# Seven half-size products in place of eight for three weight groups of a hybrid layer, with the sums done by VectorE

## What is computed

```python
h = rmsnorm(x, norm_w)
proj = jnp.matmul(h, w_in).astype(jnp.float32)     # 256x1024 times 1024x4360
...
(aq, ak, av, ag, bq, bk, bv, bg, cq, ck, cv, co, cg, ci, cf) = jnp.split(proj, cuts, axis=-1)
...
qk = jax.nn.silu(causal_dwconv(jnp.concatenate([cq, ck], axis=-1), conv_w, conv_b))
...
yc = mlstm(split_heads(cq_c, C_HEADS), split_heads(ck_c, C_HEADS), split_heads(cv, C_HEADS),
           i_pre, f_pre)
yc = yc * split_heads(jax.nn.sigmoid(co), C_HEADS)
```

## Time and profile before

| | |
|---|---|
| median of 3 runs | 1400.82 us (1400.11 to 1401.28) |
| profiled execution | 1402.55 us, span 1400.4 us |
| TensorE busy | 1197.1 us, 85% |
| VectorE busy | 604.2 us, 43% |
| ScalarE busy | 209.9 us, 15% |

### The profile page before, as it was taken

The page is one execution under the profiler, slowest core; times in us unless marked ns, Lnnn a source line. Parts: engine busy times, 40 slices in busy tenths (PEclk is TensorE's granted clock), DMA queues, the critical chain, the costliest instruction groups (busy, mean ns, idle before and its releaser), DMA issues.

```text
span 1400.4 us, 27434 instructions
## 1 busy us (share of the span) xinstructions
PE 1197.1 (85%) x10062; PEld 607.4 (43%) x10063; DVE 604.2 (43%) x1355; ACT 209.9 (15%) x474; POOL 49.4 (4%) x84
## 2 busy tenths in 40 slices
PE   7999999999999989976877779887799987878665
PEld 6757577665674433422333323333234432323222
DVE  1436333454587535433443334444354543334323
ACT  1214021130262201101110111101110110101001
POOL 0000000001011000000000000000000000000000
PEclk9999999999999999988999989999999998999888
DMA  9942177221833999999999999999979999999996
GB/s 351 282 138 91 61 280 138 78 92 59 299 145 125 380 410 418 426 429 429 427 427 430 428 428 428 426 429 428 428 306 429 429 429 428 427 430 428 429 428 288
DMA packets 63075, 467.79 MB, mean 334 GB/s; under 512 B 6848, under 2 KB 11708, under 8 KB 38460
## 3 DMA queue, kind: packets, MB, share of 16 engines
q1 hardware_dynamic: 58556, 462.49, 80.1%
q10 hardware_dynamic: 3856, 2.65, 2.3%
q0 software_dynamic: 624, 2.10, 0.4%
HBM read 465.12 MB, written 1.05 MB: 333 GB/s over the span
## 4 chain that ended last, share of the span: by engine, by line
PE 55%; DMA 34%; DVE 4%; issue 3%; SPq 2%; ACT 1%; ACTq 1%; POOLq 0%; POOL 0%; DVEq 0%
DMA ring<-in_w_up_dram 29%; PE bank L1406 18%; PE bank L978 9%; PE bank L985 7%; PE bank L1437 6%; PE bank L1154 3%; DMA ring<-in_w_down_dram 2%; PE bank L1454 2%; PE bank L1387 2%; DMA x_mem<-x_mem 1%; SPq L503 1%; PE bank L1350 1%; PE bank L1418 1%; PE bank L1211 1%; ACTq L920 1%
## 5 line engine op out<-in xcount | busy, mean ns | idle before, releaser
L1406 PE MATMUL bank<-ring,mem 128*32 128x512 f32 x2688 | 378.3, 657 | 123.0 <-DMA ring<-in_w_up_dram 100.4
L1406 PEld LDWEIGHTS bank<-ring,mem 128*32 128x32 f32 x2688 | 103.0, 119 | 306.5 <-issue 246.6
L978 PE MATMUL bank<-ring 128*128 128x256 f32 x768 | 168.7, 380 | 0.0
L1437 PE MATMUL bank<-ring,mem 128*32 128x256 f32 x2560 | 155.1, 382 | 8.4 <-DMA ring<-in_w_down_dram 7.9
L978 PEld LDWEIGHTS bank<-ring 128*128 128x128 f32 x768 | 145.1, 190 | 21.1 <-issue 1.7
L935 ACT ACTIVATE const<-bank 64x512 f32<-64x512 f32 x46 | 27.3, 594 | 795.2 <-PE bank L1406 795.2
L2440 DVE TENSOR_TENSOR mem<-bank,const 64x512 f32<-64x512 f32 x45 | 30.7, 683 | 228.5 <-PE bank L1406 228.5
L985 PE MATMUL bank<-ring 128*128 128x512 f32 (+2 forms) x320 | 123.6, 542 | 1.5 <-DVE ring L1745 1.3
L1437 PEld LDWEIGHTS bank<-ring,mem 128*32 128x32 f32 x2560 | 75.3, 109 | 77.1 <-issue 26.8
L1406 PE MATMUL bank<-x_mem,mem 128*32 128x512 f32 x256 | 69.3, 689 | 29.8 <-DMA ring<-in_w_up_dram 29.8
L985 PEld LDWEIGHTS bank<-ring 128*128 128x128 f32 x320 | 61.0, 195 | 55.8 <-issue 49.6
(11 more groups left out here) (421 smaller groups left out, 1160.5 us busy)
## 6 DMA issues: line engine op xcount, KB each, us to landing
ring<-in_w_up_dram SPq DMA_DIRECT2D x64, 2048.0 KB, 28.7
ring<-in_w_gate_dram SPq DMA_DIRECT2D x54, 2048.0 KB, 32.1
ring<-in_w_down_dram SPq DMA_DIRECT2D x53, 2048.0 KB, 26.7
ring<-in_w_in_dram SPq DMA_DIRECT2D x19, 2048.0 KB, 13.1
x_mem<-in_w_gate_dram SPq DMA_DIRECT2D x10, 2048.0 KB, 31.6
x_mem<-in_w_down_dram SPq DMA_DIRECT2D x10, 2048.0 KB, 28.3
ring<-in_w_out_dram SPq DMA_DIRECT2D x6, 2048.0 KB, 14.3
ring<-in_w_in_dram SPq DMA_DIRECT2D x2, 1056.0 KB, 6.4
```

Of the source, the lines that this page charges most:

```text
L978: i = mm(b[:, S * j:S * j + S], w[:, k, P * (c + j):P * (c + j + 1)], hT[:, k, :], start=(k == 0), stop=(k == KC - 1))
L1406: i = mm(gate_up_bank(q), xT[:, at:at + T], w[q // 2][:, c, 512 * (q % 2):512 * (q % 2 + 1)], start=(h == 0 and c == 0 and not begun), sto ...
L1437: i = mm(YB[quarter[q], 0:QD], hT_sb[:, at:at + T], w[:, c, cols_of[q]], start=(h == 0 and c == 0), stop=(h == 1 and c == 3), skip_group_c ...
```

## The change

Groups 1, 2 and 4 are each cut in halves along the tokens, the contraction and the columns of weights. The product of two such 2x2 block matrices is made with seven half-size products instead of eight (Winograd's form of Strassen's scheme). Each half-size product is 128 tokens by 512 of the contraction by 256 columns. For groups 1 and 2 it is eight matmuls that stream 128 tokens; for group 4 it is four matmuls that stream 256 columns.

VectorE makes, once a layer, four sums of halves of `hT` (`s1` to `s4`); for each group four sums of weight blocks in the ring itself (`mix`, T3, T2, T1, T4, each 128x1024 numbers) and five sums of products on their way out of PSUM (`fold`, 128x256 numbers each). ScalarE keeps three products a group (`keep`). For group 2 these operations stand inside of the gate chain. For group 4 they stand between the gate chain and the wait for the spread rows. On TensorE the first two state scores and two more pieces of group 5 change places with each other.

```diff
+SEVEN = {g: n for n, g in enumerate((1, 2, 4))}
+PRODUCTS = {name: n + 1 for n, name in enumerate(("M1", "M3", "M7", "M6", "M5", "M2"))}
+KEPT = {name: n + 1 for n, name in enumerate(("M1", "M3", "C11"))}
+FOLDED = {name: n + 1 for n, name in enumerate(("U2", "U4", "C22", "C12", "C21"))}
+MIXED = {name: n + 1 for n, name in enumerate(("T3", "T2", "T1", "T4"))}
...
+        s1, s2 = four(flat2(agT))[:, :, 0:P], four(flat2(agT))[:, :, P:S]
+        s3, s4 = four(flat2(vgB))[:, :, 0:P], four(flat2(vgB))[:, :, P:S]
+        u4 = mem3[:, 0:S]
+        products_of = {1: rawC[:, :, 3:3 + S], 2: qkA[:, 0:4, :]}
+        scale_of = {1: 1.0, 2: SCALE, 4: 1.0}
+        def corner(g, i, j):
+            if g == 4:
+                return eC[:, i, 0:S].rearrange("p (h d) -> p h d", d=HD) if j else vC[:, i, :, 0:HD]
+            return products_of[g][:, 2 * j:2 * j + 2, P * i:P * (i + 1)]
+        def chunks_of(b, g=1):
+            return b[:, 0:S].rearrange("p (c s) -> p c s", c=4 if g == 4 else 2)
+        def weights_of(g, k, n):
+            w = ring[:, g % SLOTS, :].rearrange("p (k n) -> p k n", n=512)
+            return w[:, 4 * k:4 * k + 4, S * n:S * (n + 1)]
...
+                def keep(g, product, dst, b):
+                    act.wait_ge(product_ready, seven(PRODUCTS, l, g, product))
+                    A(dst, chunks_of(b, g), ACT.Copy, scale=scale_of[g]).then_inc(kept, 1)
+                def keep_first(g):
+                    keep(g, "M1", corner(g, 1, 0), PJ[2 * g % 4])
+                    keep(g, "M3", corner(g, 0, 1), PJ[(2 * g + 1) % 4])
+                def keep_corner(g):
+                    keep(g, "M2", corner(g, 0, 0), PJ[2 * g % 4])
+                    act.sem_inc(pj_used, 2)
+                keep_first(1)
+                keep_corner(1)
+                keep_first(2)
                 arg(1)
                 result(A(rw[:, 3, :], rw[:, 2, :], ACT.Exp))
                 arg(2)
                 result(A(rw[:, 5, :], rw[:, 4, :], ACT.Ln))
-                for c in range(2):
-                    b = unit(4 + c)
-                    used(A(qkA[:, 2 * c:2 * c + 2, :], b[:, :].rearrange("p (c s) -> p c s", c=2), ACT.Copy, scale=SCALE))
-                    if c == 0:
-                        arg(3)
-                        result(A(eg[:, :, :], qkC[:, :, :], ACT.Tanh, scale=0.5))
+                keep_corner(2)
...
+                keep_first(4)
+                keep(4, "M2", corner(4, 0, 0), PJ[0])
+                for c, name in enumerate(("C12", "C22")):
+                    act.wait_ge(folded, seven(FOLDED, l, 4, name))
+                    used(A(eC[:, c, 0:S], eC[:, c, 0:S], ACT.Tanh, scale=0.5))
...
-                group(1, "T")
+                def seven_products(g):
+                    a, m, f, e = PJ[2 * g % 4], PJ[(2 * g + 1) % 4], SC[1], SC[0]
+                    hT0, hT1 = hT[:, :, 0:P], hT[:, :, P:S]
+                    def product(name, b, w, moving, first=True):
+                        for k in range(4) if g == 4 else ():
+                            i = mm(b[:, 0:S], moving[:, k, :], w[:, k, :], start=(first and k == 0), stop=(k == 3),
+                                   skip_group_check=True)
+                        for j in range(2) if g < 4 else ():
+                            for k in range(4):
+                                i = mm(b[:, P * j:P * (j + 1)], w[:, k, P * j:P * (j + 1)], moving[:, k, :],
+                                       start=(first and (j, k) == (0, 0)), stop=(k == 3), skip_group_check=True)
+                        return i.then_inc(product_ready, 1) if name in PRODUCTS else i.then_inc(pj_ready, 2)
+                    arrived(g, l * in_loads[g] + 1)
+                    if g == 1:
+                        pe.wait_ge(sc_used, l * SC_L)
+                    elif g == 2:
+                        pe.wait_ge(pj_used, l * PJ_L + 2)
+                        pe.wait_ge(folded, seven(FOLDED, l, 1, "C21"))
+                    else:
+                        pe.wait_ge(kept, seven(KEPT, l, 2, "C11"))
+                        pe.wait_ge(folded, seven(FOLDED, l, 2, "C21"))
+                    product("M1", a, weights_of(g, 0, 0), hT0[:, 0:4, :])
+                    pe.wait_ge(sums_ready, 4 * l + 3)
+                    product("M3", m, weights_of(g, 1, 1), s4)
+                    pe.wait_ge(sums_ready, 4 * l + 4)
+                    pe.wait_ge(mixed, seven(MIXED, l, g, "T3"))
+                    product("M7", f, weights_of(g, 0, 1), s3)
+                    pe.wait_ge(kept, seven(KEPT, l, g, "M3"))
+                    pe.wait_ge(mixed, seven(MIXED, l, g, "T2"))
+                    product("M6", m, weights_of(g, 0, 0), s2)
+                    pe.wait_ge(mixed, seven(MIXED, l, g, "T1"))
+                    product("M5", e, weights_of(g, 1, 1), s1)
+                    product("M2", a, weights_of(g, 1, 0), hT0[:, 4:8, :], first=False)
+                    pe.wait_ge(folded, seven(FOLDED, l, g, "C22"))
+                    pe.wait_ge(mixed, seven(MIXED, l, g, "T4"))
+                    product("M4", f, weights_of(g, 0, 1), hT1[:, 4:8, :], first=False)
+                seven_products(1)
...
-                group(2, "T")
+                seven_products(2)
+                pe.wait_ge(kept, seven(KEPT, l, 1, "C11"))
+                pe.wait_ge(folded, seven(FOLDED, l, 1, "C21"))
                 group(3, "T")
...
-                group(4, "tok")
+                seven_products(4)
                 pe.wait_ge(qkC_ready, l + 1)
                 def c_scores(heads):
                     for h in heads:
                         causal_scores(sc(h), qkC[:, 2 + h // 2, :], qkC[:, h // 2, :], HD * (h % 2)).then_inc(sc_ready, 1)
-                c_scores((0, 1))
                 slot, n = 5 % SLOTS, IN_GROUPS[5][1]
                 arrived(slot, l * in_loads[slot] + 1)
                 b, w = pj(10), slot_cols(slot, n)
                 project(b, w, 0, n, range(2))
+                pe.wait_ge(folded, seven(FOLDED, l, 4, "C21"))
+                c_scores((0, 1))
+                project(b, w, 0, n, range(2, 4))
                 c_scores((2, 3))
-                project(b, w, 0, n, range(2, KC)).then_inc(pj_ready, 1)
+                project(b, w, 0, n, range(4, KC)).then_inc(pj_ready, 1)
...
+                v.wait_ge(tr_used, l * TR_L + 5)
+                tt(s1, hT1[:, 0:4, :], hT1[:, 4:8, :], ALU.add).then_inc(sums_ready, 1)
+                v.wait_ge(sums_ready, 4 * l + 1)
+                tt(s2, s1, hT0[:, 0:4, :], ALU.subtract).then_inc(sums_ready, 1)
+                v.wait_ge(sums_ready, 4 * l + 2)
+                tt(s4, hT0[:, 4:8, :], s2, ALU.subtract).then_inc(sums_ready, 1)
+                tt(s3, hT0[:, 0:4, :], hT1[:, 0:4, :], ALU.subtract).then_inc(sums_ready, 1)
+                def mix(g, name):
+                    b11, b12 = weights_of(g, 0, 0), weights_of(g, 0, 1)
+                    b21, b22 = weights_of(g, 1, 0), weights_of(g, 1, 1)
+                    if name == "T3":
+                        v.wait_ge(w_in_slot[g], 16 * (l * in_loads[g] + 1))
+                        i = tt(b12, b22, b12, ALU.subtract)
+                    elif name == "T2":
+                        v.wait_ge(product_ready, seven(PRODUCTS, l, g, "M1"))
+                        i = tt(b11, b12, b11, ALU.add)
+                    elif name == "T1":
+                        v.wait_ge(product_ready, seven(PRODUCTS, l, g, "M3"))
+                        i = tt(b22, b22, b11, ALU.subtract)
+                    else:
+                        v.wait_ge(product_ready, seven(PRODUCTS, l, g, "M7"))
+                        i = tt(b12, b21, b11, ALU.subtract)
+                    i.then_inc(mixed, 1)
+                    v.wait_ge(mixed, seven(MIXED, l, g, name))
+                def mix_weights(g):
+                    for name in MIXED:
+                        mix(g, name)
+                def fold(g, product, dst, b, other):
+                    if product == "M4":
+                        v.wait_ge(pj_ready, l * PJ_L + PJ_0 + 2 * g + 2)
+                    else:
+                        v.wait_ge(product_ready, seven(PRODUCTS, l, g, product))
+                    return stt(out=dst, in0=chunks_of(b, g), scalar=scale_of[g], in1=other, op0=ALU.mult,
+                               op1=ALU.add).then_inc(folded, 1)
+                def fold_most(g):
+                    m, f, e = PJ[(2 * g + 1) % 4], SC[1], SC[0]
+                    v.wait_ge(kept, seven(KEPT, l, g, "M3"))
+                    fold(g, "M6", corner(g, 1, 0), m, corner(g, 1, 0))
+                    v.wait_ge(folded, seven(FOLDED, l, g, "U2"))
+                    fold(g, "M5", chunks_of(u4, g), e, corner(g, 1, 0))
+                    v.wait_ge(folded, seven(FOLDED, l, g, "U4"))
+                    fold(g, "M7", corner(g, 1, 1), f, chunks_of(u4, g))
+                    tt(corner(g, 0, 1), corner(g, 0, 1), chunks_of(u4, g), ALU.add).then_inc(folded, 1)
+                def fold_last(g):
```

(38 more changed lines are left out.)

4 lines of the change are left out of this document (1 added, 3 removed).

## The result

The changed kernel takes 1411.38 us (median of 4 runs, 1410.9 to 1412.58), the kernel before beside it 1401.05 (4 runs, 1400.11 to 1402.03). The ratio is 1.007, 95% interval 1.0057 to 1.0084: slower by 0.7%. The profiled execution took 1411.11 us, span 1408.9, for 1402.55 and 1400.4 before. So +8.5 us between the two spans, and +10.3 between the medians: the profiled execution of before was slower than each of the four runs beside the changed kernel.

What follows compares the result with a forecast made beforehand. In the layers the chain from gate chain over spreading copies to the third state score was taken to bound; from 600 us, DMA. Layer delays 2.9 and 1.8 plus clock loss 4.0 gave +8.7 us: 1409.5, range 1402 to 1418.

Steps and rivals of the forecast that it cites:

- What the products save: TensorE's groups 1, 2, 4: records 0.112 us apart, 1.3 us saved per T group, 1.75 in group 4, 8.8 in all.
- Rival (3): TensorE's T groups: narrow matmuls bound by their weight loads, 16.8 us a group, some +22 us, 1423; 8 in 100.
- What VectorE adds to the gate chain: Group 2's sums and folds inside the gate chain delay its end by 5.4 us in the first layer, 5.8 in the second.
- The copies: Spreading copies between gate chain and third state score take 21.6 us, landing at 78.9 and 247.8.
- TensorE's idle time: Ahead of the third state score TensorE idles 7.5 us in the first layer and 6.1 in the second.
- The clock: TensorE's clock falls after each layer's idle time, losing 2.0 us a stall, +4.0 for the two.
- Sum: Whole kernel: 2.9 + 1.8 + 4.0 = +8.7 us, span 1400.4 to 1409.1, median 1400.8 to 1409.5.
- Rivals (1) and (2): Shorter spreading copies: under 15 us gives 1395.5, 7 in 100; at about 17 us no change, 1399, 9 in 100.
- Rival (1): Spreading copies land early, under 15 us; VectorE's 78.8 and 249.1 then decide the third score: 1395.5; 7 in 100.

Runs made afterwards that it cites:

- the trace with fillers: Changed kernel with five matmuls on old operands, result never read, put ahead of the third state score: 1407.64 us, ratio 1.0038 to the kernel before.
- group 2 plain: Changed kernel with group 2 back at eight half-size products, groups 1 and 4 keeping seven: 1401.86 us, ratio 0.9997 to the kernel before; again 1401.47 us.

## Why the prediction was right

Forecast were 1409.5 us, in a range of 1402 to 1418, slower with a chance of 0.84. Measured were 1411.38. Step by step:

- **What the products save.** Right. Group 1 took 12.50 us, its records stand 12.50 / 112 = 0.112 us apart. Rival (3), narrow matmuls bound by their weight loads, is out. Group 4 took 73.01 - 60.82 = 12.19 us where nothing interrupted it (forecast 12.2). The 158 ns a record that I had worked out from the Trainium skill, "TensorE: Matmul & The Clock Gate", section "Back-to-back issue gap", don't hold for these matmuls.
- **What VectorE adds to the gate chain.** Right. The exponential moved by 56.76 - 51.82 = +4.9 in the first layer (forecast +5.4). In the second it moved from about 221.0 to 230.96, of which 4.1 are the later start of the layer: +5.9 (forecast +5.8).
- **The copies.** Right in the first layer, where they took 21.4 us (78.18 - 56.76) for a forecast of 21.6. They took 21.4 in the second too (252.31 - 230.96). There the prediction names 21.6 for both layers, but its landing at 247.8 is the landing of before plus 5.8, which keeps the 20.9 us of before; this is 0.4 us of the second layer's error. Landing to third score: 5.64 us in both, as in the first layer before. The second layer's rows, of ScalarE and of VectorE:

```profile
230.96 0.41 ACT L788 ACTIVATE x_mem<-x_mem 4x256 f32<-4x256 f32 x1 [6.11 <-DVE x_mem L2007]
```

```profile
252.31 0.88 DVE L2021 TENSOR_SCALAR x_mem<-x_mem,small 128x128 f32<-128x128 f32 x4 [3.66 <-DMA x_mem<-x_mem]
```

- **TensorE's idle time.** Mis-sized: 5.23 and 5.34 us for 7.5 and 6.1. In the first layer the score itself came 0.7 us sooner. The rest is TensorE coming later to it, by the 1.05 and 0.40 us behind ScalarE's held queue, and in the first layer by 0.5 us inside group 2. This came out of idle time, so the sum was untouched; the run with GpSimd's copies shows that for the queue.
- **The clock.** Right: from the third score to the last block of group 5 (`L1031 x16`) the first layer took 91.44 - 83.82 = 7.62 us, and 89.40 - 83.60 = 5.80 at full clock in the trace with fillers: 1.8 us lost, forecast 2.0. The second lost 7.60 - 5.80 = 1.8 as well. The Trainium skill, "TensorE: Matmul & The Clock Gate", section "HAM oscillation", says that an engine whose wait for a transfer is long enough is throttled again and pays the ramp each time. Behind all six waits of 4.43 to 5.92 us here the traces agree. Behind eight of 1.59 to 2.88 us the clock fell six times.
- **Sum.** +4.09 and +4.56 in the layers for a forecast of 4.9 and 3.8; together 8.65 for 8.7. The third score came at 83.82 for 84.5 in the first layer, and in the second 4.0 us later against the layer's start for 3.55. In the second layer another 0.5 us came behind the third score, since the fourth now waits for VectorE, which it did not before; the prediction had put that at nothing. That the errors of the two layers (-0.8 and +0.8) cancelled is luck. The median moved by 10.3, 1.8 more than the layers: the profiled execution of before stood 1.5 above its median. From the second layer's state sums to the end the fourteen traces take 1132.1 to 1138.7 us, whatever the layers did, so a single execution can't be held to a microsecond.
- **Rivals (1) and (2)** needed copies of 17 us or less. They took 21. Rival (1) promised 1395.5 with no copies in the way. The kernels without them came to 1398.5 and 1396.5 and pay 2.2 us a layer for the spreading; without that they would stand at 1394.1 and 1392.1, under the rival's figure, since in them the third score no longer waits for group 4's last fold either.

Not tried: whether copies that are split or smaller would land sooner, and what the new place of the first two scores among the pieces of group 5 does by itself; each kernel with seven products has it.

## What to carry to other kernels

Before an engine with slack is given more work, ask where in its program the work stands, and what follows it. VectorE was busy for 43%, and the sums of a third group cost some 10 us ahead of a 21 us transfer, while behind its start the third group gained about 3. A faster engine gains only if everything that meets it at the same point comes sooner too: with the gate chain short again, group 4's last fold came next, so list what is late next and its time before counting a gain. Do one part at a time: two of the three groups cost and gained nothing, and one carried the loss. And one trace's clock behind a short wait is a draw; repeat it before building on it.

## What the runs showed of the hardware that I had not expected

- Issuing four copies of 128 KB held ScalarE for 8.41 us in the changed kernel, one of them for 5.0 us, and for 3.42 us in the kernel before. The time differs within a kernel too: with groups 1, 3, 4 it was 3.60 us in the first layer, and in the second nearly 9 (221.54 to 230.51). What decides it is open. From GpSimd the four took 2.14 us, and the copies landed no sooner.
- Behind idle times of 4.43 to 5.92 us ahead of the third score TensorE's clock fell in each of the six cases seen, and the eight records took 4.78 to 5.77 us. Behind shorter ones it was not fixed by their length: with 1.59 us the same eight took 3.70 (twice), 5.21 or 5.40, with 1.69 us 5.16 or 5.40, with 2.63 us 4.86, with 2.88 us 6.26.
- In the first layer the gate chain begins when the gate biases land, at 35.4 to 36.4 us, whatever TensorE does. Group 1's start varied from 18.97 to 21.08 us between the traces and changes TensorE's wait at the third score. With group 2 plain it waited 2.88 us for the copies behind a start at 19.30, and 1.59 for group 4's last fold behind one at 20.80, with the score at 80.02 and 80.23.

The fastest version is that with groups 1, 3 and 4 in seven products and the rows spread by TensorE: 1396.50 us, ratio 0.9962 (0.9949 to 0.9976) to the kernel before.
